# Reordering the unit pipeline of two attentions: transpositions and copies in front of the scores, outputs in the bank of the second transposed tile

## The chip, the cores and the metric

One NeuronCore of a Trainium2 chip runs the whole program. The metric is the device time of one execution in microseconds. The engines named here are TensorE (PE for its matmuls and PEld for its weight loads in the profile), VectorE (DVE), ScalarE (ACT), GpSimd (POOL) and SyncE (SP).

## The reference, cut to what matters

The program is one block of recurrent branches with a feed-forward part, and then two attention layers, all over 1024 tokens of width 1024 in 32-bit floats. The change touches two attentions of these layers: attention B (8 query heads on 2 key heads of width 64) and attention C (8 heads of width 96, values of width 64). Both are plain softmax attention over blocks of 128 queries:

```python
def one(qi):
    s = jnp.einsum('bqhgd,bkhd->bhgqk', qi, k).astype(jnp.float32) * scale
    p = jax.nn.softmax(s, axis=-1).astype(v.dtype)
    return jnp.einsum('bhgqk,bkhd->bqhd', p, v)
```

Attention D, in the second layer after C, subtracts one softmax from another. It isn't touched; the change gives B and C its order of work.

## The kernel before, in words

Attentions B and C each have 32 units. A unit b is a pair of heads (m = 0 and 1) at one block of 128 queries; 8 units in a row belong to one pair of heads p. For a unit there is this work:

- **S(b,0), S(b,1)**: TensorE makes the scores, 128 x 1024 each, in two banks of PSUM (line 1095 in B, line 1104 in C).
- VectorE takes the largest score of a row (line 2905) and makes a bias of it (helper, line 2167). ScalarE writes exp(scores) to SBUF (line 2061), which frees the bank of that S. VectorE takes the reciprocal of the sum (line 2925) and scales the probabilities (helper, line 2163, counted in `s_probs`).
- **T(b,0), T(b,1)**: TensorE transposes the probabilities, 8 tiles of 128 x 128 for each head (line 1126). ScalarE copies both to the tiles A(20) and A(21) (line 2071), which frees their banks.
- **O(b)**: TensorE multiplies values with A(20) and A(21), 32 small matmuls in one bank (line 1115). VectorE multiplies the result with the gate (helper, line 2159), which frees the bank.

There are four banks (`PS[0]` to `PS[3]`), given out in turn: the n-th job that TensorE opens (`opn`) takes bank n % 4 and must wait until the job n-4 was freed. `filled[i]` and `freed[i]` count per bank. Every engine takes its instructions strictly in the order of its own text, so the order of jobs sets both who shares a bank and who is queued behind whom.

Step s of the loop in `attend_pairs` does, before the change, on TensorE: S(s,0), S(s,1), O(s-2), T(s-1,0), T(s-1,1), so five jobs; on ScalarE: exp(s,0), exp(s,1), copy T(s-1,0), copy T(s-1,1); on VectorE: the maxima of S(s), the multiplication of O(s-2), the reciprocals and scalings of s. There are 34 steps.

`weave(main, side)` puts one piece of other work behind each step, on each engine. In B these are the projections of the next pair of heads (`prep_b`: behind steps 0, 8 and 16 a product `qb`; behind steps 1, 9 and 17 a rotation, a sum of squares `hq` and the product `gb` for the gate, all of `three`, line 336, but for the small ones) and behind steps 26 to 33 one eighth each of an output projection (`heads_out`, line 353, whose result VectorE adds to H in `half_in`, line 2159). Steps 2 to 7, 10 to 15 and 18 to 25 have nothing beside them on TensorE: 20 plain steps. In C every step up to 30 has side work: six times four pieces of `prep_c` (a product `qc`; `hq` with, for h = 4 and 6, the gate's product `gc`, and then a product `kc`; a sum `hn`; a spreading `hb`, with the product `vc` for even h), then seven pieces of `prep_d` (`qd`; `hq` and `kd`; `hn`; `hb`; `vd`; its transposition; `gd`). On ScalarE, a piece with a gate loads a table before the Silu and another one after it (lines 1832 and 1335), `kc` is followed by a copy, a square, and a copy and a square of the shared key (lines 1958 to 1965), `qc` by a copy, a square and two DMA issues, `qd` and `kd` by a copy, a square and four DMA issues (lines 1734, 1736, 1728, 1729). Ahead of the first unit of each pair of heads, `ready(p)` in C also waits until the keys of that pair were finished on VectorE, out of the bank of `hb`.

The order of TensorE around one step before:

```python
for s in range(nu + 2):
    if s < nu:            # S(s,0), S(s,1)
...
    if s >= 2:            # O(s-2), waits for both copies of T(s-2)
...
    if 1 <= s < nu + 1:   # T(s-1,0), T(s-1,1), each waits for s_probs
```

Of the kernel before, what the change touches and what calls it, by code (L numbers as in the profile page):

```python
# [11 lines left out]
ACT = mybir.ActivationFunctionType  # L12
AX = mybir.AxisListType

P = 128
# [3 lines left out]
NT = L // P  # L19
# [41 lines left out]
def build(nc, a):  # L61
    with ExitStack() as ctx:
# [26 lines left out]
        PS = [ctx.enter_context(nc.psum_tensor(f"ps{i}", [P, L], F32)) for i in range(4)]  # L89
        def sem(name):  # L90
            return ctx.enter_context(nc.semaphore(name))
# [79 lines left out]
        s_low_in = sem("low_in")  # L171
        s_kraw = sem("kraw")
        s_od_done = sem("od_done")
        s_turned = sem("turned")
        s_turned_out = sem("turned_out")
        s_lamv = sem("lamv")
# [4 lines left out]
        def A(i):  # L181
            return AR[:, i, :]
# [25 lines left out]
        J = {}  # L208
# [6 lines left out]
        def bank(name):  # L215
            return J[name] % 4

        def turn(name):
            return J[name] // 4 + 1
# [54 lines left out]
        def _(pe):  # L274
            def opn(name):
                n = njobs[0]
                njobs[0] += 1
                assert name not in J, name
                J[name] = n
                return PS[n % 4], n  # L280
# [790 lines left out]
            def att_a():  # L1071
# [2 lines left out]
                    pe.wait_ge(s_vs_in, 32 * (p + 1))  # L1074
                return attend_windows(ready)

            def attend_pairs(kind, q, k, v, ready):

                base = BASE[kind] = cnt["unit"]
                first = cnt["prob"]  # L1080
                nu = 32
                for s in range(nu + 2):
                    if s < nu:
                        b, p, u = base + s, s // 8, s % 8
                        if u == 0:
                            ready(p)
                        rows = slice(u * P, u * P + P)
                        if kind == "B":
                            two = [opn(("S", b, m)) for m in range(2)]
                            for pt, n in two:  # L1090
                                pe.wait_ge(freed[n % 4], n // 4)
                            for h in range(2):
                                for m, (pt, n) in enumerate(two):
                                    e = slice(m * 64, m * 64 + 64)
                                    mm = pe.matmul(pt[:, h * 512:h * 512 + 512], q(p, m)[e, rows],  # L1095
                                                   k(p, m)[e, h * 512:h * 512 + 512], start=True, stop=True)
                                    if h:
                                        mm.then_inc(filled[n % 4], 1)
                        else:
                            for m in range(2):  # L1100
                                pt, n = opn(("S", b, m))
                                pe.wait_ge(freed[n % 4], n // 4)
                                for h in range(2):
                                    mm = pe.matmul(pt[:, h * 512:h * 512 + 512], q(p, m)[0:96, rows],  # L1104
                                                   k(p, m)[0:96, h * 512:h * 512 + 512], start=True, stop=True)
                                mm.then_inc(filled[n % 4], 1)
                    if s >= 2:
                        b, p = base + s - 2, (s - 2) // 8
                        for m in range(2):
                            pe.wait_ge(freed[bank(("T", b, m))], turn(("T", b, m)))  # L1110
                        pt, n = opn(("O", b))
                        pe.wait_ge(freed[n % 4], n // 4)
                        for c in range(NT):
                            for m in range(2):
                                mm = pe.matmul(pt[m * 64:m * 64 + 64, 0:P], v(p, c, m), A(20 + m)[:, c * P:c * P + P],  # L1115
                                               start=c == 0, stop=c == NT - 1)
                        mm.then_inc(filled[n % 4], 1)
                    if 1 <= s < nu + 1:
                        b = base + s - 1
                        for m in range(2):  # L1120
                            pe.wait_ge(s_probs, first + 2 * (s - 1) + m + 1)
                            pt, n = opn(("T", b, m))
                            pe.wait_ge(freed[n % 4], n // 4)
                            pr = PROB[kind][(2 * (s - 1) + m) % 4]
                            for c in range(NT):
                                mm = pe.transpose(pt[:, c * P:c * P + P], pr[:, c * P:c * P + P], IDENT)  # L1126
                            mm.then_inc(filled[n % 4], 1)
                    yield
                cnt["unit"] += nu
                cnt["prob"] += 2 * nu  # L1130
# [192 lines left out]
        def _(act):  # L1323
            done = {}

            def tick(sem):
                done[sem.name] = done.get(sem.name, 0) + 1
                return done[sem.name]
# [720 lines left out]
            def attend_pairs(kind, scale):  # L2049
                base = cnt["unit"]  # L2050
                nu = 32
                for s in range(nu + 2):
                    if s < nu:
                        b = base + s
                        for m in range(2):
                            i = (2 * s + m) % 4
                            if s >= 2:
                                act.wait_ge(filled[bank(("T", b - 2, m))], turn(("T", b - 2, m)))
                            cnt["s"] += 1
                            act.wait_ge(s_negmax, cnt["s"])  # L2060
                            act.activation(PROB[kind][i], PS[bank(("S", b, m))][:, :], ACT.Exp, scale=row_scale(kind, s, m),  # L2061
                                           bias=SM[:, 20 + i:21 + i], accum_out=SM[:, 24 + i:25 + i])\
                                .then_inc(freed[bank(("S", b, m))], 1)
                            act.wait_ge(freed[bank(("S", b, m))], turn(("S", b, m)))
                    if 1 <= s < nu + 1:
                        b = base + s - 1
                        if s >= 2:
                            act.wait_ge(filled[bank(("O", b - 1))], turn(("O", b - 1)))
                        for m in range(2):
                            act.wait_ge(filled[bank(("T", b, m))], turn(("T", b, m)))  # L2070
                            act.activation(A(20 + m), PS[bank(("T", b, m))][:, :], ACT.Copy)\
                                .then_inc(freed[bank(("T", b, m))], 1)
                            act.wait_ge(freed[bank(("T", b, m))], turn(("T", b, m)))
                    yield
                cnt["unit"] += nu

# [1105 lines left out]
```

## Time and profile before

| what | value |
|---|---|
| device time, median of 3 runs | 3973.64 us (3968.29, 3973.64, 3984.16) |
| the profiled execution's own time | 3979.41 us |
| its span | 3977.6 us |
| TensorE busy | 3764.0 us, 95% of the span |
| VectorE busy | 1844.3 us, 46% |
| ScalarE busy | 1296.7 us, 33% |
| GpSimd busy | 914.3 us, 23% |
| granted TensorE clock, mean | 0.973 of full speed |
| attention B, first scores to last output | 2593.7 to some 2921 us of the span |
| attention C, first scores to last output | 3082.6 to 3476.9 us of the span |

A row of the timeline is: start, duration, engine, line, operation, output<-input, shapes and count, and in square brackets the idle time of the engine before it with what ended it. Matmuls are pipelined, so a group's duration runs a little into the next group's start; the distance from start to start is what a group costs TensorE. In a waits row, the instruction on the left waited for the one on the right: total, number of times, longest.

### The profile page before, as it was taken

How to read it: one execution, taken by the hardware profiler on the slowest of the kernel's cores; microseconds unless marked ns; L12 is line 12 of the kernel's file. 1: busy time of each engine (PE TensorE's matmuls, PEld its weight loads, DVE VectorE, ACT ScalarE, POOL GpSimd, SP SyncE). 2: the span in 40 equal slices, each digit the busy share in tenths (PEclk: the TensorE clock that was granted, in tenths of full speed). 3: DMA queues.
4: the chain of work that ended last, by engine and by line, in shares of the span. 5: the costliest groups of instructions: out<-in, count | busy, mean ns of one | idle time of the engine just before them, and what ended most of it. 6: DMA issues, size and time to landing. Idle time of an engine off the chain costs nothing.

```text
span 3977.6 us, 51609 instructions
## 1 busy us (share of the span) xinstructions
PE 3764.0 (95%) x21680; PEld 2965.5 (75%) x21680; DVE 1844.3 (46%) x2312; ACT 1296.7 (33%) x1520; POOL 914.3 (23%) x558
## 2 busy tenths in 40 slices
PE   7999999999999999999999899999999999988888
PEld 6778888877788778888888677767676566666667
DVE  7464555524733621101103556655744655465472
ACT  3244333332330011000001244455624665433341
POOL 4212222222233424333333311110022001111001
PEclk8999999999999999999999999999999999998899
DMA  4111111111125421111113211100121001010011
GB/s 138 37 43 51 46 53 44 49 53 46 48 87 191 124 85 48 48 48 48 48 50 110 82 42 48 37 18 10 51 84 32 14 12 40 19 25 19 16 54 66
DMA packets 276811, 215.30 MB, mean 54 GB/s; under 512 B 16272, under 2 KB 255024, under 8 KB 276592
## 3 DMA queue, kind: packets, MB, share of 16 engines
q1 hardware_dynamic: 256656, 146.11, 13.0%
q10 hardware_dynamic: 19936, 66.07, 4.6%
q8 instruction: 162, 2.65, 0.3%
q14 instruction: 57, 0.47, 0.0%
HBM read 170.27 MB, written 37.81 MB: 52 GB/s over the span
## 4 chain that ended last, share of the span: by engine, by line
PE 82%; DVE 10%; ACT 4%; issue 2%; ACTq 1%; DMA 0%; DVEq 0%; SPq 0%
PE ps L336 33%; PE ps L353 17%; PE ps L384 12%; DVE AR L2159 3%; PE ps L1104 2%; DVE SM L2905 2%; PE ps L603 2%; PE ps L318 2%; DVE AR L2167 2%; PE ps L1184 1%; PE ps L1115 1%; PE ps L1095 1%; PE ps L429 1%; PE ps L1126 1%; PE ps L295 1%
## 5 line engine op out<-in xcount | busy, mean ns | idle before, releaser
L3029 POOL CAST WH<-WR 128x1024 fp32r<-128x1024 f32 (+2 forms) x269 | 280.1, 1041 | 2925.8 <-DMA WR<-in_w_in 832.3
L3031 POOL TENSOR_TENSOR WL<-WR,WH 128x1024 fp32r<-128x1024 f32 (+2 forms) x269 | 595.6, 2214 | 21.6
L336 PE MATMUL ps<-XH,WH 128*128 128x512 f32 (+1 forms) x1968 | 499.2, 396 | 2.3 <-DVE AR L2159 1.7
L336 PE MATMUL ps<-XH,WL 128*128 128x512 f32 (+1 forms) x1968 | 488.8, 391 | 0.0
L336 PE MATMUL ps<-XL,WH 128*128 128x512 f32 (+1 forms) x1968 | 486.3, 389 | 0.0
L336 PEld LDWEIGHTS ps<-XH,WH 128*128 128x128 f32 (+1 forms) x1968 | 366.0, 188 | 86.6 <-issue 5.7
L336 PEld LDWEIGHTS ps<-XH,WL 128*128 128x128 f32 (+1 forms) x1968 | 369.3, 188 | 80.5
L336 PEld LDWEIGHTS ps<-XL,WH 128*128 128x128 f32 (+1 forms) x1968 | 367.1, 187 | 79.2
L2159 DVE TENSOR_TENSOR AR<-AR 128x512 f32<-128x512 f32 (+3 forms) x336 | 379.2, 1128 | 53.4 <-ACT AR L1593 38.0
L353 PE MATMUL ps<-ARR,WH 128*128 128x512 f32 x1600 | 396.1, 390 | 8.2 <-ACT ARR L1690 4.8
L353 PEld LDWEIGHTS ps<-ARR,WH 128*128 128x128 f32 x1600 | 300.5, 188 | 72.5 <-ACT ARR L1690 5.5
L2159 DVE TENSOR_TENSOR AR<-AR,ps 128x1024 f32<-128x1024 f32 (+2 forms) x72 | 84.7, 1176 | 544.8 <-PE ps L336 409.3
L2905 DVE TENSOR_REDUCE SM<-ps 128x1 f32<-128x1024 f32 x128 | 156.8, 1225 | 196.8 <-PE ps L1104 116.0
L2167 DVE SCALAR_TENSOR_TENSOR AR<-ps,AR 128x512 f32<-128x512 f32 (+2 forms) x122 | 59.3, 486 | 347.8 <-ACT AR L1348 239.7
L1708 ACT ACTIVATE AR<-ps 128x1024 f32<-128x1024 f32 x22 | 22.6, 1027 | 558.4 <-PE ps L336 558.4
L353 PE MATMUL ps<-ARR,WL 128*128 128x512 f32 x736 | 189.4, 392 | 0.0
L384 PE MATMUL ps<-XH,WH 128*128 128x512 f32 x672 | 185.7, 421 | 1.6 <-ACT AR L2002 1.6
L2061 ACT ACTIVATE AR<-ps,SM,AR 128x1024 f32<-128x1024 f32 x112 | 135.1, 1206 | 154.0 <-DVE SM L2167 147.8
L2163 DVE TENSOR_SCALAR AR<-AR,SM 128x1024 f32<-128x1024 f32 (+2 forms) x209 | 174.0, 833 | 7.3
L384 PE MATMUL ps<-XH,WL 128*128 128x512 f32 x672 | 167.3, 391 | 0.0
L384 PE MATMUL ps<-XL,WH 128*128 128x512 f32 x672 | 166.0, 389 | 0.0
L353 PEld LDWEIGHTS ps<-ARR,WL 128*128 128x128 f32 x736 | 139.3, 189 | 29.0
(254 smaller groups left out, 5135.9 us busy)
## 6 DMA issues: line engine op xcount, KB each, us to landing
WR<-in_w_in SPq DMA_DIRECT2D x78, 512.0 KB, 3.8
WR<-in_w_ffn_in SPq DMA_DIRECT2D x44, 512.0 KB, 3.8
spill<-H ACTq DMA_DIRECT2D x32, 512.0 KB, 2.7
gates<-AR ACTq DMA_DIRECT2D x32, 512.0 KB, 2.8
AR<-gates SPq DMA_DIRECT2D x32, 512.0 KB, 4.0
H<-spill ACTq DMA_DIRECT2D x32, 512.0 KB, 5.5
WR<-in_w_in_e SPq DMA_DIRECT2D x26, 512.0 KB, 3.9
WR<-in_w_in_o SPq DMA_DIRECT2D x23, 512.0 KB, 3.8
```

Of the source, the lines that this page charges most:

```text
L318: pe.matmul(pt[:, h * 512:h * 512 + 512], wp[:, slot, k, :], XH[:, k, h * 512:h * 512 + 512], start=k == 0 and wp is WH, stop=False, skip_ ...
L336: mm = pe.matmul(pt[0:m, h * 512:h * 512 + 512], wp[:, slot, k, 0:m], xp[:, k, h * 512:h * 512 + 512], start=i == 0, stop=i == 3 * KD - 1)
L353: mm = pe.matmul(pt[:, h * 512:h * 512 + 512], wp[:, w % 4, k, :], xp(k)[:, h * 512:h * 512 + 512], start=i == 0, stop=i == 3 * nk - 1)
L384: mm = pe.matmul(pt[:, h * 512:h * 512 + 512], wp[:, w % 4, k, :], xp[:, k, h * 512:h * 512 + 512], start=i == 0, stop=i == 3 * KD - 1)
L603: mm = pe.matmul(out, x1[r, c], later, start=True, stop=True)
L2061: act.activation(PROB[kind][i], PS[bank(("S", b, m))][:, :], ACT.Exp, scale=row_scale(kind, s, m), bias=SM[:, 20 + i:21 + i], accum_out=SM ...
L2159: return v.tensor_tensor(o, x, y, op)
L2163: return v.tensor_scalar(o, x, s1, None, op0)
L2167: return v.scalar_tensor_tensor(out=o, in0=x, scalar=s, in1=y, op0=op0, op1=op1)
L2905: v.tensor_reduce(SM[:, 34 + m:35 + m], PS[bank(("S", b, m))][:, :], AX.X, ALU.max)\
L3029: pool.tensor_copy(hi, full).then_inc(s_whi, 1)
L3031: pool.tensor_tensor(lo, full, hi, ALU.subtract).then_inc(s_wsplit, 1)
```

## The change

On TensorE, step s of `attend_pairs` now does T(s-2,0), T(s-2,1), S(s,0), S(s,1), O(s-2): the transpositions of the unit two back come first, and O(s-2) is written in the bank that T(s-2,1) had, after ScalarE copied it. So a step opens four jobs, not five. On ScalarE the two copies of T(s-2) come ahead of the exps of step s. VectorE's text is the same. Two new semaphores, `s_pair_turned` and `s_pair_out`, tell of T(b,1) and its copy, since that bank's own counters now belong to O(b). The transpositions are no longer made in step s-1; steps 32 and 33 have T and O of the last two units.

```diff
@@ TensorE, attend_pairs
+                    if s >= 2:
+                        b = base + s - 2
+                        for m in range(2):
+                            pe.wait_ge(s_probs, first + 2 * (s - 2) + m + 1)
+                            pt, n = opn(("T", b, m))
+                            pe.wait_ge(freed[n % 4], n // 4)
+                            pr = PROB[kind][(2 * (s - 2) + m) % 4]
+                            for c in range(NT):
+                                mm = pe.transpose(pt[:, c * P:c * P + P], pr[:, c * P:c * P + P], IDENT)
+                            mm.then_inc(s_pair_turned if m else filled[n % 4], 1)
+                        J[("O", b)] = J[("T", b, 1)]
                     if s < nu:
...
                     if s >= 2:
                         b, p = base + s - 2, (s - 2) // 8
-                        for m in range(2):
-                            pe.wait_ge(freed[bank(("T", b, m))], turn(("T", b, m)))
-                        pt, n = opn(("O", b))
-                        pe.wait_ge(freed[n % 4], n // 4)
+                        pe.wait_ge(freed[bank(("T", b, 0))], turn(("T", b, 0)))
+                        pairs_out[0] += 1
+                        pe.wait_ge(s_pair_out, pairs_out[0])
+                        pt = PS[bank(("O", b))]
...
-                        mm.then_inc(filled[n % 4], 1)
-                    if 1 <= s < nu + 1:
-                        b = base + s - 1
-                        for m in range(2):
-                            pe.wait_ge(s_probs, first + 2 * (s - 1) + m + 1)
-                            pt, n = opn(("T", b, m))
-                            pe.wait_ge(freed[n % 4], n // 4)
...
-                            mm.then_inc(filled[n % 4], 1)
+                        mm.then_inc(filled[bank(("O", b))], 1)
@@ ScalarE, attend_pairs
+                    if s >= 2:
+                        b = base + s - 2
+                        if s >= 3:
+                            act.wait_ge(filled[bank(("O", b - 1))], turn(("O", b - 1)))
+                        act.wait_ge(filled[bank(("T", b, 0))], turn(("T", b, 0)))
+                        act.activation(A(20), PS[bank(("T", b, 0))][:, :], ACT.Copy)\
+                            .then_inc(freed[bank(("T", b, 0))], 1)
+                        act.wait_ge(freed[bank(("T", b, 0))], turn(("T", b, 0)))
+                        act.wait_ge(s_pair_turned, done.get("pair_out", 0) + 1)
+                        act.activation(A(21), PS[bank(("T", b, 1))][:, :], ACT.Copy).then_inc(s_pair_out, 1)
+                        act.wait_ge(s_pair_out, tick(s_pair_out))
                     if s < nu:
...
-                            if s >= 2:
-                                act.wait_ge(filled[bank(("T", b - 2, m))], turn(("T", b - 2, m)))
...
-                    if 1 <= s < nu + 1:
-                        b = base + s - 1
-                        if s >= 2:
-                            act.wait_ge(filled[bank(("O", b - 1))], turn(("O", b - 1)))
-                        for m in range(2):
-                            act.wait_ge(filled[bank(("T", b, m))], turn(("T", b, m)))
-                            act.activation(A(20 + m), PS[bank(("T", b, m))][:, :], ACT.Copy)\
-                                .then_inc(freed[bank(("T", b, m))], 1)
```

## Rows read from the trace of the kernel before

**Rows 1.** Busy time by stretch (attention B, attention C): each engine, clock, DMA.

```profile
2593.70:2908.00 314.30, 294.82 (x2197) 214.36 (x2198) 199.26 (x325) 175.75 (x221) 27.22 (x24) 1.00 0.08 26
3082.50:3478.00 395.50, 376.69 (x2554) 255.11 (x2556) 217.41 (x368) 218.13 (x277) 34.02 (x20) 0.99 0.09 21
```

**Rows 2.** Waits of TensorE in the stretch of attention B.

```profile
PE ps L1095 <- ACT AR L2061: 5.9, 20, 0.5
PE ps L1126 <- ACT AR L2061: 4.9, 15, 0.4
```

**Rows 3.** Waits of TensorE in the stretch of attention C.

```profile
PE ps L1104 <- issue: 6.2, 4, 1.5
```

**Rows 4.** Timeline of one plain step of attention B.

```profile
2646.13 2.08 ACT L2071 ACTIVATE AR<-ps 128x1024 f32<-128x1024 f32 x2
2646.15 1.99 PE L1095 MATMUL ps<-AR 64*128 64x512 f32 x8 [0.30 <-ACT AR L2061]
...
2648.24 1.22 DVE L2905 TENSOR_REDUCE SM<-ps 128x1 f32<-128x1024 f32 x1 [1.09 <-PE ps L1095]
...
2648.31 1.97 PE L1115 MATMUL ps<-AR 128*64 128x128 f32 x32 [0.17 <-issue]
...
2650.21 2.07 PE L1126 MATMUL ps<-CST,AR 128*128 128x128 f32 x16
...
2651.15 0.29 DVE L2159 TENSOR_TENSOR AR<-ps,AR 128x128 f32<-128x128 f32 x1
2651.23 1.21 ACT L2061 ACTIVATE AR<-ps,SM,AR 128x1024 f32<-128x1024 f32 x1 [0.16 <-DVE SM L2167]
...
2652.58 1.99 PE L1095 MATMUL ps<-AR 64*128 64x512 f32 x8 [0.30 <-ACT AR L2061]
```

**Rows 5.** Timeline of a step of attention B with an output product behind it.

```profile
2852.81 1.07 PE L1126 MATMUL ps<-CST,AR 128*128 128x128 f32 x8 [0.45 <-ACT AR L2061]
...
2854.18 1.21 PE L353 MATMUL ps<-XH,WH 128*128 128x512 f32 x4 [0.30 <-ACT AR L2061]
...
2859.89 1.99 PE L1095 MATMUL ps<-AR 64*128 64x512 f32 x8
2860.06 1.22 DVE L2159 TENSOR_TENSOR H<-H,ps 128x1024 f32<-128x1024 f32 x1 [3.56 <-PE ps L353]
```

**Rows 6.** Timeline of attention B, TensorE alone: scores of units 8 and 11.

```profile
2665.63 1.99 PE L1095 MATMUL ps<-AR 64*128 64x512 f32 x8 [0.50 <-ACT AR L2061]
...
2710.88 1.99 PE L1095 MATMUL ps<-AR 64*128 64x512 f32 x8 [0.17 <-ACT AR L2061]
```

**Rows 7.** Timeline of attention C behind a gate's product and a key's product.

```profile
3194.96 1.28 ACT L1832 ACT_TABLE_LOAD   x1 [10.45 <-PE ps L336]
...
3196.64 3.70 PE L1104 MATMUL ps<-AR 96*128 96x512 f32 x8
...
3197.30 1.28 ACT L1335 ACT_TABLE_LOAD   x1
...
3201.87 1.05 ACT L1965 ACTIVATE AR<-AR 32x1024 f32<-32x1024 f32 x1
...
3205.72 1.09 PE L411 MATMUL ps<-AR,CST 96*64 96x128 f32 x16 [0.26 <-ACT AR L2061]
```

**Rows 8.** Timeline of attention C, TensorE alone: a key's step, a new pair.

```profile
3239.48 3.70 PE L1104 MATMUL ps<-AR 96*128 96x512 f32 x8
3243.11 1.97 PE L1115 MATMUL ps<-AR 128*64 128x128 f32 x32
...
3247.46 1.09 PE L411 MATMUL ps<-AR,CST 96*64 96x128 f32 x16 [0.39 <-ACT AR L2061]
...
3258.61 3.67 PE L1104 MATMUL ps<-AR 96*128 96x512 f32 x8 [1.54 <-issue]
```

**Rows 9.** Timeline of attention C, ScalarE alone: a DMA issue behind `kd`.

```profile
3399.17 0.63 ACTq L1728 DMA_DIRECT2D AR<-AR  x1
```

**Rows 10.** Busy time by stretch, as in rows 1: during the scores of unit 3 of C.

```profile
3109.70:3113.50 3.80, 3.80 (x7) 1.71 (x6) 0.88 (x3) 0.78 (x3) 0.00 (x0) 0.50 0.01 4
```

More of the change, by code:

```diff
@@ L173, in build @@
         s_od_done = sem("od_done")
+        s_pair_turned = sem("pair_turned")
+        s_pair_out = sem("pair_out")
         s_turned = sem("turned")
@@ L1075, in att_a @@
                 return attend_windows(ready)
+            pairs_out = [0]
             def attend_pairs(kind, q, k, v, ready):
@@ L1116, in attend_pairs @@
                                                start=c == 0, stop=c == NT - 1)
-                        mm.then_inc(filled[n % 4], 1)
-                    if 1 <= s < nu + 1:
-                        b = base + s - 1
-                        for m in range(2):
-                            pe.wait_ge(s_probs, first + 2 * (s - 1) + m + 1)
-                            pt, n = opn(("T", b, m))
-                            pe.wait_ge(freed[n % 4], n // 4)
-                            pr = PROB[kind][(2 * (s - 1) + m) % 4]
-                            for c in range(NT):
-                                mm = pe.transpose(pt[:, c * P:c * P + P], pr[:, c * P:c * P + P], IDENT)
-                            mm.then_inc(filled[n % 4], 1)
+                        mm.then_inc(filled[bank(("O", b))], 1)
                     yield
@@ L2064, in attend_pairs @@
                             act.wait_ge(freed[bank(("S", b, m))], turn(("S", b, m)))
-                    if 1 <= s < nu + 1:
-                        b = base + s - 1
-                        if s >= 2:
-                            act.wait_ge(filled[bank(("O", b - 1))], turn(("O", b - 1)))
-                        for m in range(2):
-                            act.wait_ge(filled[bank(("T", b, m))], turn(("T", b, m)))
-                            act.activation(A(20 + m), PS[bank(("T", b, m))][:, :], ACT.Copy)\
-                                .then_inc(freed[bank(("T", b, m))], 1)
-                            act.wait_ge(freed[bank(("T", b, m))], turn(("T", b, m)))
                     yield
```

## The prediction

> **What bounds the kernel now.** I read the page first: TensorE is busy for 95% of the span, and the chain that ended last is for the most part its matmuls. So a change of order can only give back time in which TensorE stands still in the two stretches that it touches. The busy time by stretch sizes that: in attention B 314.30 us with 294.82 busy, 19.5 us idle; in attention C 395.50 with 376.69 busy, 18.8 us idle [rows 1]. Together 38.3 us, 1% of the span. That is the ceiling of any gain.
>
> Next the waits of TensorE by stretch, to see who ends the idle time. In B they end with the exp (line 2061): 20 waits of the scores and 15 of the transpositions, of 0.5 us at most [rows 2]. In C the largest group is four waits of the scores of 1.5 us each, put down to issue [rows 3]; by their place three of them are `ready(p)`, which waits until VectorE has scaled the keys out of the bank of `hb` [rows 8].
>
> Then the timeline of one plain step of B, which is as regular as a clock: scores start at 2646.15 and again at 2652.58, so 6.43 us [rows 4]. TensorE's own work, from start to start, is 2.16 (scores, 1.92 where they come without a wait) + 1.90 (outputs) + some 1.80 to 1.85 (16 transpositions), 5.9 us. The rest is the end of a loop that runs scores (filled at 2.0), maximum 0, maximum 1, exp 1 (5.08 to 6.29 after the start), and then the next scores, which need the bank of exp 1. That loop sets the plain step, not TensorE.
>
> **The change, part by part.** Nothing is computed more or less often; only waits move. I write times from the start of the scores of a step, or from the end E of the side work, and follow who waits for which bank by counting jobs: four per step now, plus the side ones.
>
> *Plain steps of B, 20 of them.* The loop scores, maxima, exp 1, scores is not touched, since S(s+1,1) takes the bank of S(s,1) and, with four jobs, S(s+1,0) that of S(s,0). What is new lies inside it: TensorE does O(s-2) from 2.16 to 4.06, T(s-1,0) to 4.96, and T(s-1,1) must wait until VectorE has multiplied O(s-2), whose bank it takes. VectorE comes to that behind the two maxima, at 5.00 to 5.29 [rows 4]. So T(s-1,1) runs from about 5.35 to 6.25, and the scores come at 6.43 as before. The copies start when exp 1 has ended, as now, and end at 2.06 of the next step, in time for O at 2.16. Cost 0: the idle time is only split in two. The cover is thin, 0.2 us; if it fails, every tenth costs 2 us over these steps.
>
> *Steps 26 to 31 of B, with an output product behind them.* Before, the second transposition waits 0.45 us for exp 0 and the product 0.30 for exp 1 [rows 5], and from 2847.46 to 2859.89 (the scores before and behind) a step takes 12.43 us. With the new order the product takes the bank of T(s-2,0), long free, and the transpositions behind it find everything ready; S' needs the bank of the product, which VectorE empties at 0.17 + 1.22 us behind its end [rows 5], under the 1.80 of the transpositions. The step becomes 1.92 + 1.90 + 5.71 (2854.18 to 2859.89) + 1.80 = 11.33. Gain 1.1 x 6 = 6.6 us. In the last two steps there are no scores between T and O any more, so O waits for both copies: transpositions end at 1.8, copy 1 at about 3.15 (each is half of 2.08 us). Loss 1.35 x 2 = 2.7 us.
>
> *Steps with `qb` and `gb` in B.* Units 8 to 11 take 2710.88 - 2665.63 = 45.25 us [rows 6]. In the new order the waits for exp in front of `qb` and the rotation go. For them: behind `qb`, S' needs its bank, free after ScalarE's copy and square, 0.75 us later than the transpositions end; behind `gb` the Silu with its table load (1.28 + 1.02) keeps the bank 0.8 us longer than they cover, and the second load (1.28 [rows 7]) and the two copies then stand ahead of O, another 1.4 us. Walked through to the same point: 45.7 us, 0.45 more. Three such pairs, the first a little cheaper: +1.1 us.
>
> B in sum: -6.6 + 2.7 + 1.1 = -2.8 us.
>
> *C, where the copies come behind ScalarE's side work.* Here the moved copies have a price. The scores take 3.63 us, outputs 1.90 [rows 8], transpositions 1.80: 7.33 of work a step, above the loop of 6.4, so bare steps don't wait. Behind side work TensorE now reaches O at E + 1.8 + 3.6 = E + 5.4, and the copies (2.1 us) start only when ScalarE has done its part of the side work:
> - `qc` (copy, square, two DMA issues, 3.5 us): copies done at 5.8, stall 0.4; five such steps: +2.0, before none.
> - `kc` without a gate (copy, square, copy, square, some 4.5 us): done at 6.6, stall 1.2, four times.
> - `kc` behind a gate's product: ScalarE is through at 3201.87 + 1.05 = 3202.92, 6.3 us behind the start of the scores [rows 7]; stall E + 8.4 against 5.4 = 3.0, twice.
>  So 4 x 1.2 + 2 x 3.0 = 10.8. Before, the same six places take, from the scores to the `hn` behind them, 7.98 (twice, as 3239.48 to 3247.46 [rows 8]), 9.08 (twice, 3196.64 to 3205.72 [rows 7]), 9.47 and 9.98; less 7.33 each, 9.6 us of waits. Net +1.2.
> - `qd`, `kd`: copy and square, 2.2 us, and four DMA issues of 0.63 and a little [rows 9], 4.9 us; copies done at 7.0, stall 1.6 twice. `hn` behind them: 0.15, since VectorE's rotations get 1.8 us more. Together 3.35 against 4.1 before (8.55, 7.96 and 9.57 less 7.33). Net -0.75.
> - `ready(p)`: 1.54 us before [rows 8]; now the transpositions come first, but the scaling of the keys stands behind the second scaling of the probabilities, and about 0.9 is left. Three times: -1.9.
> - Steps 31 to 33: O(30) and O(31) wait for their copies before (1.50 and 1.42) and after; with the gate `gd` ahead, +0.3.
>
> C in sum: 2.0 + 1.2 - 0.75 - 1.9 + 0.3 = +0.85 us.
>
> *The rest.* Weight loads hang on the end of the product four back (SP's queue), whose order is the same and whose distances change by about a microsecond. GpSimd's splits follow them. Attention D and what follows start from the same state.
>
> **Sum.** -2.8 + 0.85 = -2.0 us. The profiled execution took 3979.41 us (span 3977.6); it would take 3977.4. It lies 5.8 us over the median of its three runs, so against the median I forecast 3973.6 - 2.0, about **3972 us**.
>
> **A row and a rule on the clock.** During the scores of unit 3 of C the granted clock was 0.50, the lower of its two levels, for 3.80 us; TensorE had just stood still, or nearly, for 1.4 us and 0.4 us [rows 10]. The eight matmuls took 6.16 us where others take 3.70. It fell once more, behind a 1.54 us wait at 3355, and not behind the other waits of that size. I count as many falls after as before. The Trainium skill (TensorE: Matmul & The Clock Gate, section Part 1: The HAM clock gate) says that the clock is lowered after idle stretches and only sustained activity brings the full rate back; the trace agrees at that place. By that rule alone the longer stalls of 3.0 us would each cost more than the stall, which speaks against this change; that is a rival below.
>
> **Rivals.**
> 1. *The waits really go.* If the copies and multiplications came in time everywhere, B and C would have no idle time: 38.3 us less, 3935 us. For it: the products of steps 26 to 31 do lose their waits. Against it: the plain steps are bound by a loop that the change leaves alone, and the copies stand behind ScalarE's side work. It would count from half of the ceiling on. Chance 0.07.
> 2. *The stalls lower the clock (slower).* Mechanism: O waits for late copies, TensorE idles, and the scores and products that follow run at half rate. There are 13 new or kept stalls of 1.2 us and more (five in B, eight in C). A fall costs half of the 3.80 us of [rows 10], 1.9 us: 13 x 1.9 = 25 us, so 3997 us. It decides from about 11 falls on. Against it: of four waits of 1.5 us in C only one was followed by a fall. Chance 0.05.
> 3. *T(s-1,1) behind the multiplication lengthens each step (slower).* If the wait on VectorE pushed the scores back by 0.5 us in the 60 steps, 30 us, 4002 us. Against it: 0.2 us of room in B by [rows 4], over 1 us in C. Chance 0.03.
>
> My forecast, waits that change places with no difference to be measured, has 0.85.
>
> **Range.** Its lower end: 3972 less 4 (no fall of the clock), less 6 (the stalls for copies, some 18 us in sum, a third smaller), less 5 (the spread of the runs before, 3968 to 3984, around its median): 3957. Its upper end: 6 for stalls a third larger, 6 for three more falls, and 6 for the spread: 3990. The rivals lie outside, with 0.15 in all. A measurement of this kernel tells about 0.5% from no change, 20 us: faster by more, 0.07 (rival 1); slower by more, 0.08 (rivals 2 and 3); within, 0.85.
>
> **What would show it.** Right: plain steps of B at 6.43 us, with T(s-1,1) waiting about 0.4 us for line 2159; steps 26 to 31 at 11.3; outputs (line 1115) that wait for line 2071 in C, 3 us behind both gates; idle time of TensorE in the two stretches within 5 us of 38.3. Wrong: plain steps above 6.6 (rival 3), a clock well under 0.98 in either stretch (rival 2), or idle time under 20 us (rival 1).

## The result and the profile after

| | before | after |
|---|---|---|
| device time, median of 18 runs each | 3973.57 us (3953.04 to 3984.16) | 3979.6 us (3975.33 to 3996.27) |
| the profiled execution, its span | 3979.41, 3977.6 us | 3977.78, 3976.0 us |

The ratio is 1.0028, with a 95% interval of 1.0015 to 1.0040: the changed kernel is slower by about 11 us by that ratio (the two medians lie 6.0 us apart, the two means 10.3), where 2 us less were forecast. The median lies in the range of the forecast, but its sign is wrong. The bound of 0.5% that the prediction gave for what can be told from no change was too wide: 18 runs of each resolve half of it.

The two profiled executions are a trap, for by them the new order is 1.6 us faster. Attention B begins at 2593.72 us of the span before and at 2587.60 after. That is 6.1 us ahead of any changed instruction, and more than the effect. So I compare stretches, each from its own first matmul. They are shown as [rows 1] are (window, length, busy time of each engine, granted clock, DMA). The three rows are attention B up to the first scores of C, C up to the first scores of D, and the rest.

```profile
2587.60:3077.99 490.39, 453.67 (x3059) 341.40 (x3059) 269.97 (x401) 232.66 (x285) 71.88 (x54) 0.98 0.13 39
3077.99:3477.33 399.34, 372.37 (x2549) 255.80 (x2549) 212.39 (x367) 218.11 (x277) 33.93 (x20) 0.99 0.09 21
3477.33:3976.00 498.67, 431.89 (x2394) 333.50 (x2392) 272.30 (x407) 172.59 (x227) 59.70 (x48) 0.94 0.12 36
```

The same three stretches of the kernel before:

```profile
2593.72:3082.58 488.86, 458.05 (x3059) 338.41 (x3059) 272.77 (x401) 232.73 (x285) 73.44 (x54) 0.98 0.12 39
3082.58:3476.86 394.28, 375.55 (x2548) 254.41 (x2549) 217.12 (x367) 218.13 (x277) 34.02 (x20) 0.99 0.09 21
3476.86:3977.60 500.74, 434.47 (x2394) 336.13 (x2392) 271.16 (x407) 172.59 (x227) 59.42 (x48) 0.93 0.12 36
```

B is 1.5 us longer, C 5.1 us, and the rest, which has the same text in both, is 2.1 us shorter. The idle time of TensorE (length less busy) went from 30.8 to 36.7 us in B and from 18.7 to 27.0 in C, 14 us more in the two together; since the busy time fell by 7.6 us, the two stretches grew by 6.6 us only. The prediction asked for less than 5 us of difference; its sign for a lost clock, a granted clock well under 0.98 in either stretch, did not show in this profile (0.98 and 0.99).

The changed kernel has other line numbers. 1095 is the transposition, 1110 and 1119 are the scores of B and of C, 1130 is the output product O. On ScalarE, 2063 and 2067 are the copies of the two transposed tiles, 2075 is exp, and 1741, 1837 and 1965 are the square behind a projection, the gate's Silu and the shared key's square. On VectorE, 2164 and 2172 are helpers.

Who ends the idle time is in the waits of TensorE, first for B and then for C (line after, line waited for: total, times, longest). They answer to [rows 2, 3].

```profile
PE ps L1130 <- ACT AR L2067: 14.2, 11, 1.5
PE ps L1095 <- DVE AR L2164: 4.2, 12, 0.5
PE ps L1110 <- ACT AR L1837: 3.1, 4, 0.8
PE ps L1110 <- ACT AR L1741: 1.3, 2, 0.7
...
PE ps L1130 <- ACT AR L2067: 21.7, 16, 2.7
PE ps L1119 <- ACT AR L2063: 2.5, 3, 0.9
PE ps L1119 <- DVE AR L2172: 1.8, 1, 1.8
```

The waits for exp are gone, as forecast. In their place O waits for the second copy (line 2067). The rows of B end at 2908 of the span, and one more such wait, of 1.47 us, follows at 2915.04. In sum there are 28 of them with 37 us, and 12 of the 28 are in B, where the forecast had five.

The timeline of B (start, duration, engine, line, operation, what ended the idle time before it) has them. The first row is the second transposition of a plain step. Then come the scores and outputs behind a gate; then step 19 with ScalarE's work around it, and the scores of step 26; then the scores of steps 27, 28 and 31 and the output of step 32:

```profile
2639.98 1.06 PE L1095 MATMUL ps<-CST,AR 128*128 128x128 f32 x8 [0.30 <-DVE AR L2164]
...
2699.30 1.99 PE L1110 MATMUL ps<-AR 64*128 64x512 f32 x8 [0.82 <-ACT AR L1837]
2702.70 1.97 PE L1130 MATMUL ps<-AR 128*64 128x128 f32 x32 [1.41 <-ACT AR L2067]
2706.49 1.99 PE L1110 MATMUL ps<-AR 64*128 64x512 f32 x8
...
2784.23 0.82 ACTq L1381 DMA_DIRECT2D H<-spill  x2
2785.06 1.99 PE L1110 MATMUL ps<-AR 64*128 64x512 f32 x8
2785.09 1.06 ACT L2107 ACTIVATE XH<-AR 128x1024 fp32r<-128x1024 f32 x1 [0.89 <-ACT AR L2075]
2786.18 1.02 ACT L2063 ACTIVATE AR<-ps 128x1024 f32<-128x1024 f32 x1
2787.23 1.02 ACT L2067 ACTIVATE AR<-ps 128x1024 f32<-128x1024 f32 x1
2788.40 1.97 PE L1130 MATMUL ps<-AR 128*64 128x128 f32 x32 [1.35 <-ACT AR L2067]
...
2833.74 1.99 PE L1110 MATMUL ps<-AR 64*128 64x512 f32 x8
...
2846.26 1.99 PE L1110 MATMUL ps<-AR 64*128 64x512 f32 x8
2857.52 1.99 PE L1110 MATMUL ps<-AR 64*128 64x512 f32 x8
...
2891.39 1.99 PE L1110 MATMUL ps<-AR 64*128 64x512 f32 x8
2904.17 1.97 PE L1130 MATMUL ps<-AR 128*64 128x128 f32 x32 [1.47 <-ACT AR L2067]
```

The rows at 2784 to 2788 are the ones to learn from. ScalarE issues two DMAs and rounds a tile of 1024 columns (line 2107) that a later product needs, and then copies. That rounding stands behind the exps, and so ahead of the next step's copies, in seven of the steps 18 to 25 (step 24 has none), and the two DMA issues stand ahead of it in the first four. Before the change the copies stood ahead of it. O then waits 1.35 to 1.44 us in steps 19 to 22, 0.50 in 23, 1.21 in 24, not at all in 25, behind the step without a rounding, and 1.21 in 26. From the scores of step 19 (2785.06) to those of step 26 (2833.74) a step takes 6.95 us. The same scores before the change, 6.68 us a step:

```profile
2788.58 1.99 PE L1095 MATMUL ps<-AR 64*128 64x512 f32 x8 [0.32 <-ACT AR L2061]
...
2835.34 1.99 PE L1095 MATMUL ps<-AR 64*128 64x512 f32 x8 [0.30 <-ACT AR L2061]
```

From 2857.52 to 2891.39 three steps take 11.29 us each, as forecast.

In C: O behind `qc`, O behind `kc`, the scores of `ready(p)`; behind a gate and `kc` the second half of the scores and O, and the same O one pair of heads later; O behind `qd` and behind `kd`, and the scores behind `hn` of the second layer:

```profile
3129.16 1.97 PE L1130 MATMUL ps<-AR 128*64 128x128 f32 x32 [0.61 <-ACT AR L2067]
3141.55 1.97 PE L1130 MATMUL ps<-AR 128*64 128x128 f32 x32 [1.35 <-ACT AR L2067]
3155.45 3.67 PE L1119 MATMUL ps<-AR 96*128 96x512 f32 x8 [0.84 <-ACT AR L2063]
3191.25 1.98 PE L1119 MATMUL ps<-AR 96*128 96x512 f32 x4 [0.47 <-ACT AR L1965]
3195.62 2.84 PE L1130 MATMUL ps<-AR 128*64 128x128 f32 x32 [2.39 <-ACT AR L2067]
3294.14 1.97 PE L1130 MATMUL ps<-AR 128*64 128x128 f32 x32 [2.39 <-ACT AR L2067]
3375.37 1.97 PE L1130 MATMUL ps<-AR 128*64 128x128 f32 x32 [2.66 <-ACT AR L2067]
3397.49 3.30 PE L1130 MATMUL ps<-AR 128*64 128x128 f32 x32 [2.06 <-ACT AR L2067]
3407.44 3.10 PE L1119 MATMUL ps<-AR 96*128 96x512 f32 x4 [1.83 <-DVE AR L2172]
```

**The clock** shows in these rows too. The same 32 matmuls took 2.84 us behind one wait of 2.39 us and 1.97 behind another. The granted clock (last column but two) in five such places:

```profile
3195.62:3198.18 2.56, 2.56 (x32) 2.56 (x34) 0.00 (x0) 2.48 (x4) 0.00 (x0) 0.68 0.00 0
3294.14:3296.04 1.90, 1.90 (x35) 1.90 (x37) 0.00 (x0) 1.87 (x3) 0.00 (x0) 1.00 0.00 0
3375.37:3377.26 1.89, 1.89 (x32) 1.72 (x32) 0.00 (x0) 1.86 (x3) 0.00 (x0) 1.00 0.05 9
3397.49:3400.52 3.03, 3.03 (x33) 3.03 (x35) 0.24 (x1) 2.48 (x4) 0.22 (x1) 0.57 0.02 5
3407.44:3410.48 3.04, 3.04 (x5) 0.83 (x5) 1.95 (x4) 0.89 (x1) 0.00 (x0) 0.62 0.00 0
```

Three of these five waits of 1.8 to 2.7 us were followed by the low level, and two were not, among them the longest.

**Two terms of every run.** Each run has its span and mean granted clock. At the low of its two levels the granted clock is 0.50 [rows 10], so a run lost about span x (1 - clock) to it, and its device time less that is its time at full clock. This is an estimate, since time in which TensorE waits at the low clock costs nothing; a straight line through the 87 runs below gives 0.94 us of device time for each us so counted. Over 87 runs of the kernel before, which were made beside the experiments, the time at full clock scatters by 2.5 us (standard deviation), the raw time by 6.5. This separates waits from clock for every kernel below, with a standard error of 0.7 us for 12 runs. What is lost to the clock scatters as the raw time does, and its mean over 12 runs has an error of 1.9 us:

| kernel (runs) | mean us | at full clock, against before | lost to the clock |
|---|---|---|---|
| before (87) | 3969.9 | 3872.9 | 97.0 |
| after (18) | 3982.6 | +7.8 | 102.0 |
| e1, B alone (12) | 3972.8 | +3.0 | 97.0 |
| e2, C alone (12) | 3982.4 | +4.0 | 105.5 |
| e3, O in its own bank (12) | 3985.7 | +6.5 | 106.2 |
| e4, side piece ahead, B 26 to 33 (12) | 3968.1 | -2.3 | 97.5 |
| e5, the same, 26 to 30 (11) | 3965.8 | -4.4 | 97.3 |
| e6, C's copies on VectorE (12) | 3972.4 | +0.6 | 98.9 |
| e7, e5 and e6 (12) | 3970.7 | -3.4 | 101.2 |
| e8, rounding behind copies (10) | 3976.5 | +3.1 | 100.6 |
| e10, e5 and C's key pieces (12) | 3960.9 | -7.7 | 95.7 |

So of the 12.7 us between these means, 7.8 are longer waits and 5.0 are more time at the low clock. The 7.8 are firm. The 5.0 are uncertain by some 2 us: against the 18 runs of the kernel before that belong to its own comparison the changed kernel is 10.3 us slower in the mean, not 12.7.

### The profile page after: what moved, and what is told of

Its sections match the earlier page's. It is cut to its first block, busy times and chain, and to the rows that moved or that the text cites. A ratio compares the mean times of both kernels' runs of the same rounds, so it can differ in the third digit from the quotient of the medians.

```text
span 3976.0 us, 51608 instructions
## 1 busy us (share of the span) xinstructions
PE 3751.8 (94%) x21680; PEld 2965.8 (75%) x21680; DVE 1834.0 (46%) x2312; ACT 1296.5 (33%) x1520; POOL 915.0 (23%) x558
## 4 chain that ended last, share of the span: by engine, by line
PE 84%; DVE 7%; ACT 6%; issue 1%; ACTq 1%; DMA 0%; DVEq 0%; SPq 0%
PE ps L338 33%; PE ps L355 17%; PE ps L386 12%; PE ps L1130 2%; DVE AR L2164 2%; PE ps L605 2%; PE ps L320 2%; PE ps L1119 2%; PE ps L1095 1%; DVE AR L2172 1%; PE ps L1189 1%; PE ps L1110 1%; PE ps L297 1%; PE ps L431 1%; DVE SM L2910 1%
## 5 line engine op out<-in xcount | busy, mean ns | idle before, releaser
L1130 PEld LDWEIGHTS ps<-AR 128*64 128x64 f32 x2048 | 114.1, 139 | 87.5 <-issue 87.5
L2168 DVE TENSOR_SCALAR AR<-AR,SM 128x1024 f32<-128x1024 f32 (+2 forms) x209 | 162.1, 776 | 7.3
```

Of the source, the lines that this page charges most:

```text
L2168: return v.tensor_scalar(o, x, s1, None, op0)
```

## The experiments

Line numbers of T, O and the copies shift in some of these kernels; what each is, is said. "At full clock" for a stretch is its length less half of its time at the low clock.

### Which of the two attentions: e1 and e2

Each keeps the old text for one attention and the new one for the other:

```diff
-            def attend_pairs(kind, q, k, v, ready):     # one order for both
+            def attend_pairs_b(kind, q, k, v, ready):   # e1: new order; e2: old order
+            def attend_pairs_c(kind, q, k, v, ready):   # e1: old order; e2: new order
```

> Attention B in the new order, attention C in the old one. From the two traces, the stretch from the first scores of B to the last output product beside it is 327.3 us before and 329.3 us after; C is 394.3 and 399.3. Theory 1 (late copies on ScalarE are what costs, most of it in C): B alone gives +2 us, stretch of B 329.3, stretch of C 394 as before; 3975 to 3976 in time. Theory 2 (the second transposition, which waits on VectorE's multiplication because it gives its bank to the outputs, costs in each step): most of the 6 to 11 us lies in B, which has its waits in nearly all steps; stretch of B above 331. Theory 3 (the extra time is in neither stretch, but in the clock of attention D and of what follows): both single changes are the same as before in their stretches.

> Attention C in the new order, B in the old one. Theory 1: +5 us, stretch of C 399 us against 394.3, with outputs (line of the 32 small matmuls) waiting 1.35 us behind each kc, 2.4 us behind each gate, 2.1 to 2.7 us behind qd and kd; time 3978 to 3980. Theory 2: C gains or stays, since it has more than 1 us of room for the multiplication. Theory 3: stretch 394 to 395, and the time still above before.

Measured: B alone 3974.23 us, ratio 1.0010 (0.9994 to 1.0027); C alone 3982.98 us, ratio 1.0028 (1.0015 to 1.0041). C alone has the ratio of the whole change, and B alone can't be told from no change by its raw time. C alone costs clock, 8.5 us (with an error of 2), and B none. At full clock the two add 3.0 and 4.0 us, 7.0 of the 7.8. In the profile of e1, B has the same 329.3 us as in the changed kernel, as its first theory had it. The stretch of C in the profile of e1 (old order) and of e2 (new order):

```profile
3081.76:3471.41 389.65, 372.16 (x2549) 253.30 (x2549) 216.06 (x367) 217.96 (x277) 34.01 (x20) 1.00 0.09 22
```

```profile
3077.60:3483.27 405.67, 378.41 (x2548) 259.62 (x2549) 212.82 (x367) 217.94 (x277) 33.91 (x20) 0.97 0.09 21
```

16 us lie between them, of which 10 are the clock (0.97 against 1.00): at full clock C takes 393.9 with the new order and 388.0 with the old.

### Is it the shared bank: e3

O gets a bank of its own again, in the new order, so that a step opens five jobs:

```diff
-                            mm.then_inc(s_pair_turned if m else filled[n % 4], 1)
-                        J[("O", b)] = J[("T", b, 1)]
+                            mm.then_inc(filled[n % 4], 1)
...
-                        pt = PS[bank(("O", b))]
+                        pt, n = opn(("O", b))
+                        pe.wait_ge(freed[n % 4], n // 4)
```

> Both attentions in the new order, but the outputs in a bank of their own (five jobs a step again), so that the second transposition no longer waits for VectorE's multiplication of the outputs before. Theory 1: about the time of the changed kernel, 1 us less at most (plain steps of B 6.43 us in place of 6.47); the waits of the outputs for ScalarE's copies stay, 1.35 and 2.4 us in C. Theory 2: the extra time goes, 3973 us, ratio 1.000 to the kernel before.

Measured: 3986.35 us, ratio 1.0037 (1.0023 to 1.0051). At full clock 1.3 us under the changed kernel, hardly more than the error of 0.9 us. Behind the gate in C the same waits stand, 0.47 and 2.34 us:

```profile
3196.18 1.98 PE L1173 MATMUL ps<-AR 96*128 96x512 f32 x4 [0.47 <-ACT AR L2019]
3200.51 1.97 PE L1184 MATMUL ps<-AR 128*64 128x128 f32 x32 [2.34 <-ACT AR L2150]
```

So the outputs over the second transposed tile cost next to nothing, and it is the order that costs.

### Where the gain of steps 26 to 31 comes from: e4 and e5

The old order everywhere, but in B the side piece comes ahead of the transpositions, in steps 26 to 33 (e4) or 26 to 30 (e5):

```diff
+                    ahead = kind == "B" and 26 <= s < 31     # e4: s >= 26
+                    if ahead:
+                        yield
                     if 1 <= s < nu + 1:                      # T(s-1,0), T(s-1,1)
...
-                    yield
+                    if not ahead:
+                        yield
```

> The kernel before, with one thing of the new order: in steps 26 to 33 of B the output product is put ahead of the transpositions of the same step (scores, outputs, product, transpositions). My reading of the gain that the new order has in these steps is that the product and the transpositions behind it no longer wait for exps; then a step takes 11.3 us in place of 12.4, six times, and the last two steps don't stall on copies: 7 us less than before, 3966 to 3967 us, ratio 0.998. Rival: the gain comes from the four-job rotation of the banks, or the product now waits for the bank of a transposed tile; then steps stay above 12 us.

> The kernel before, with the output product ahead of the transpositions only in steps 26 to 30 of B. In the run with steps 26 to 33, the steps of 26 to 31 were 11.3 us as expected, but the outputs of steps 32 and 33 each waited 1.42 us, since the transpositions then stood right in front of them. My theory: with five steps and the last three as before, all of the gain of 1.2 us a step stays, 6 us in the stretch of B (321 us against 327.3), time 3965 to 3967. Rival: the gain of the earlier run was within the noise and this one is 1.000 too.

Measured: e4 3967.32 us, ratio 0.9996 (0.9981 to 1.0010); e5 3965.67 us, ratio 0.9989 (0.9978 to 0.9999). By these intervals e4 can't be told from no change and e5 barely can; their times at full clock, 2.3 and 4.4 us under the kernel before, and the profiles can. A step with an output product takes 11.3 us in both, as with the new order. In e4 both last outputs then wait for copies made too late, as in the changed kernel and against what was expected, so that the gain is a third of the 7 us (waiter L1119 is O there):

```profile
2916.04 1.97 PE L1119 MATMUL ps<-AR 128*64 128x128 f32 x32 [1.42 <-issue]
```

Leaving the last steps as they were (e5) gives 2.1 us of that back, by the times at full clock, and B from its first scores to the product behind its last output takes 321.6 us where 321 was expected. So the gain of the forecast, 6.6 less 2.7 us, needs none of the rest of the change; it comes from the product standing between the exps and the transpositions.

### Is it ScalarE's queue: e6, e7, e8 and e9

e6 has the old order in B and the new one in C, with C's copies made by VectorE; e7 adds e5:

```diff
-                        act.activation(A(20), PS[bank(("T", b, 0))][:, :], ACT.Copy)
+                        v.tensor_copy(A(20), PS[bank(("T", b, 0))][:, :])
```

> B as before; C in the new order, but VectorE copies the transposed tiles, ahead of its maxima, in place of ScalarE. Theory 1 (the outputs wait because the copies stand behind ScalarE's side work): the waits of the outputs behind qc (0.61 us, five), kc (1.35, four), the gates (2.4, two), qd and kd (2.1 to 2.7) go for the most part, and C, 394 us at full clock in the changed kernel and 388 to 389 before, comes down to some 380 us; time 3962 to 3966, ratio 0.998 or less. VectorE's rotations behind kc leave a wait of about 0.5 us. Rival (the order itself costs, by the bank shared with the outputs or by VectorE's multiplication): C stays at 394 us or above, and VectorE, with 2.3 us more a step, makes it longer still: 3983 and more.

> The two together: B in the old order with the product ahead in steps 26 to 30, C in the new order with VectorE's copies. If both hold, their gains add up: 6 + 8 = 14 us or more less than before, 3958 us, ratio 0.9965. If C with VectorE's copies is no gain, it is as long as the worse of the two plus or minus the 6 us of B.

Measured: e6 3970.99 us, ratio 1.0010 (0.9998 to 1.0023); e7 3970.75 us, ratio 1.0003 (0.9993 to 1.0013). The output behind the gate waits no more:

```profile
3191.05 1.98 PE L1174 MATMUL ps<-AR 96*128 96x512 f32 x4 [0.47 <-ACT AR L2020]
3192.97 1.97 PE L1185 MATMUL ps<-AR 128*64 128x128 f32 x32
```

Of the 4.0 us that the new order costs in C at full clock, 3.4 are gone (e2 against e6, with an error of 1). But more was expected, C at some 380 us: it takes 389.4 us at full clock, no less than with the old order, for the waits moved. In e6 nine outputs wait 9.4 us for VectorE's copies, 3.6 the longest (a tenth, with 1.70, follows behind the window of these rows), and the scores of `ready(p)` wait as long as in the old order:

```profile
PE ps L1185 <- DVE AR L2989: 9.4, 9, 3.6
PE ps L1174 <- issue: 6.0, 4, 1.5
```

No kernel with C in the new order beat the same kernel with C in the old one: e7 took 3970.75 us and not the 3958 that was hoped for, and is slower than e5.

e8 is the changed kernel with ScalarE's side piece (the rounding, line 2107) behind the exps moved behind the copies of the next step, in steps 18 to 25 of B:

```diff
                         act.wait_ge(s_pair_out, tick(s_pair_out))   # the two copies are made
+                    if kind == "B" and s >= 19:
+                        yield
...
-                    yield
+                    if kind != "B" or s < 18:
+                        yield
```

> The changed kernel, with one thing moved on ScalarE in B: from step 18 on its side work (the rounding copies of steps 18 to 25, 1.06 us each) runs between the two copies of the transposed tiles and the exps of the next step, where ScalarE is idle, in place of ahead of the copies. My forecast forgot these rounding copies. Theory: steps 18 to 25, 6.95 us on average in the changed kernel, come back to 6.47, 3.5 to 4 us less in B, and the outputs there wait no longer for ScalarE. Rival: the exps are now late, and the steps stay at 6.9 or more.

Measured: 3976.33 us, ratio 1.0020 (1.0003 to 1.0037); at full clock 4.7 us under the changed kernel. In the profile the stretch from B's first scores to C's is 4.2 us shorter at full clock (single profiles of one text differ there by up to 2.6 us). A step from 19 to 25 takes 6.64 us on average (6.95 in the changed kernel, 6.47 expected), and step 26 takes 11.43 in place of 12.52. O starts without a wait, and only the second transposition waits for VectorE. Three rows, T(s-1,1), S and O:

```profile
2786.30 1.06 PE L1095 MATMUL ps<-CST,AR 128*128 128x128 f32 x8 [0.52 <-DVE AR L2167]
2787.37 1.99 PE L1110 MATMUL ps<-AR 64*128 64x512 f32 x8
2789.48 1.97 PE L1130 MATMUL ps<-AR 128*64 128x128 f32 x32
```

e9 is the changed kernel with every gate a plain copy, so that ScalarE loads no tables around it. It leaves out the Silu of all gates:

```diff
-                act.activation(dst, PS[bank(name)][:, :], other(ACT.Silu)).then_inc(freed[bank(name)], 1)
+                act.activation(dst, PS[bank(name)][:, :], ACT.Copy).then_inc(freed[bank(name)], 1)
```

> The changed kernel, with every gate computed by a plain copy in place of the Silu, so that ScalarE loads no tables around a gate (it leaves out the Silu of all gates). If what the gates add in the new order is ScalarE's queue (function tables and gate ahead of the copies of the transposed tiles), then in C the output products behind the two gates wait for the copies 1.35 us (as behind a key's copy without a gate) in place of 2.39, and the 0.47 of the second scores goes: 1.5 us twice, C 3 us shorter at full clock, about 391. In B the waits of 0.82 and 1.41 us behind each of the three gates go: 6.6 us, and B about 484. Rival: the waits are not ScalarE's queue but VectorE's multiplies, and stay within 0.3 us of what they were.

Measured, one run: 3983.71 us, at a mean clock of 0.971. The waits of C came as expected, 1.35 us behind both gates and no wait of the scores; at full clock C takes 390.4 us (391 expected). In B the waits of 0.82 and 1.41 us are gone as well, but units 8 to 11 shorten by 1.52 us only (46.05 to 44.53), not 2.2, since 0.52 us of a wait for VectorE comes up behind them. B as a whole, up to the first scores of C, is 3.3 us shorter at full clock, half of the 6.6 expected. The total is higher than the changed kernel's, but the clock took some 115 us of this run, against 102 there; at full clock the run is 12 us under the changed kernel. It is one run, and other gates of the program lose their tables too. The output behind the first gate of C:

```profile
3201.69 1.97 PE L1130 MATMUL ps<-AR 128*64 128x128 f32 x32 [1.35 <-ACT AR L2067]
```

### What beats both: e10

e5 for B, and C in the old order with the side piece ahead of the transpositions in steps 7, 15 and 23, where `hb` of the next pair is made (the recorded text calls B's order new in steps 26 to 31; it is the old one with the product put ahead, as in e5):

```diff
-                    ahead = kind == "B" and 26 <= s < 31
+                    ahead = 26 <= s < 31 if kind == "B" else s in (7, 15, 23)
```

> Attention B as in the kernel with the new order in steps 26 to 31 alone plus the old order elsewhere, as in the fifth experiment, and in C, in the old order, the side piece ahead of steps 7, 15 and 23 is put in front of the transpositions. If the wait of 1.54 us in which the scores behind a scaled key wait is only VectorE's chain begun too late, it falls to about 0.6 us in the three places: C 2.8 us shorter at full clock (386 to 387), total some 8 us under the kernel before, ratio about 0.998. Rivals: the wait stays at 1.5 us because the key piece is set by the other scaling; or C is shorter at full clock and the gain is lost in more time at the low clock (ratio 0.999 to 1.000).

Measured: 3960.84 us, ratio 0.9979 (0.9965 to 0.9994), about 8 us under the kernel before. The scores of `ready(p)` wait 0.98, 0.98 and 0.85 us, where 0.6 was expected and [rows 8] have 1.54; of 2.8 us hoped for 1.8 came. Two rows, the transpositions, now behind the side piece, and the scores of the new pair:

```profile
3150.42 1.97 PE L1192 MATMUL ps<-CST,AR 128*128 128x128 f32 x16
3153.37 3.67 PE L1167 MATMUL ps<-AR 96*128 96x512 f32 x8 [0.98 <-issue]
```

At full clock C takes 386.8 us, 1.9 less than the mean of four profiles with the old order (388.7); the clock took no more than before.

## Why the prediction was wrong, point by point

**B, forecast -2.8 us, measured +2.0** from the first scores to the product behind the last output (327.3 to 329.3 us; e1 has the same 329.3).
- *Plain steps, "Cost 0".* This is the first step that failed: "The copies start when exp 1 has ended, as now". For the bare steps it holds: 6.46 us against 6.43, with the second transposition 0.30 us behind line 2164, where 0.4 was forecast. But of the 20, seven of the steps 18 to 25 are not bare on ScalarE. Their rounding of 1.06 us, in four of them with two DMA issues, now stands ahead of the copies, and the cover of 0.2 us that I called thin fails: O waits 1.35 to 1.44 us behind the four, and 0.50 to 1.21 behind the other three. A step takes 6.95 us against 6.68, +1.9 us in seven of them, and step 26, whose copies come behind the last rounding, keeps 12.52 us and gains nothing: 1.2 us of forecast gain missed. e8 takes the rounding out of the way, and 4.7 us at full clock come back. I had looked at what stood beside these steps on TensorE, and not at ScalarE's own side pieces.
- *Steps with an output product, 11.33 us.* Right: 11.23 to 11.38. The steps from 27 on gained 1.25 us each (four of them took 45.13 us in place of 50.12). e4 and e5 show that the mechanism was the one named.
- *The last two steps, 2.7 us.* 2.9 (1.47 twice).
- *`qb` and `gb`, 0.45 us a pair.* 0.80 (45.25 to 46.05): the waits are the ones forecast, 0.67 behind `qb` (0.75), 0.82 and 1.41 behind `gb` (0.8 and 1.4), but less of the old idle time went.

**C, forecast +0.85 us, measured +5.3 at full clock** (388.7 to 393.9, means of four profiles each). Of the 4.4 us between:
- *`qd`, `kd` and the `hn` behind, "stall 1.6 twice" and "0.15".* Mis-sized, the largest term: 2.66, 2.06 and 1.83, together 6.55 against 3.35, so 3.2 us. One DMA issue behind `qd` took 1.19 us where [rows 9] have 0.63, and one had taken 1.18 there before the change. Behind `kd` all four took 0.63, and still O came 7.4 us behind the start of the transpositions (3390.09 to 3397.49) where 7.0 were reckoned. VectorE finishes with `hn`'s bank only behind three rotations of 3.75 us in sum, while the scores that want it come early.
- *`qc`, 0.4.* 0.61, five times: 1.05 us.
- *`kc`, 1.2 and 3.0.* Right: 1.35 four times and 0.47 + 2.39 twice, 11.1 us against 10.8. e9 confirms the 1.5 us of the tables.
- *`ready(p)`, 0.9.* Right: 0.84 and 0.85 (twice).
- *Steps 31 to 33, +0.3.* 0.8: three outputs wait 0.76, 1.47 and 1.47 us, where two waited 1.50 and 1.42.

**The clock, "I count as many falls after as before".** This step failed as well, and it makes 5.0 of the 12.7 us. In one profile each of before and after the low clock in C does last equally long, 10.2 us. But over five profiles with the new order and ScalarE's copies in C (after, e2, e3, e8, e9) it lasted 10.2, 23.6, 17.1, 10.2 and 27.0 us, over five with the old order (before, e1, e4, e5, e10) 10.2, 3.4, 13.4, 10.2 and 3.4. The means differ by 9.5 us, worth half of it in time, 4.7; with values that scatter so, five on each side give the sign and not the size. The runs agree: the clock takes nothing more with B alone, 8.5 us more with C alone. Rival 2 had the mechanism, and no more than a fifth of its 25 us came. Its price of 1.9 us a fall was too low for the fall that it was read from: there the clock stayed at 0.50 for 6.8 us, of which [rows 10] show 3.80, so that fall was worth 3.4 us. The rule of the Trainium skill (TensorE: Matmul & The Clock Gate, section Part 1: The HAM clock gate) that idle stretches lower the clock agrees with this in its direction; two of the five waits above were followed by no fall. No run changed the length of these waits alone. That their length brings the falls is argued from e2 against e6, where the clock's share falls from 105.5 to 98.9 us with the waits (101.2 in e7), and not shown: each share has an error of 1.9 us, and in the profiles of e6 and e7 the low clock in C lasts 13.7 and 16.7 us, hardly less than the 17.6 of the five.

**In sum**: 4.8 us missed in B, 4.4 in C and 5.0 from the clock make 14.2 of the 14.7 us between the forecast of -2.0 and the +12.7 of the means. (By the comparison of 18 runs each, with +10.3 us, the clock's part would be 2 to 3 us.) The forecast took "waits that change places" for a balance without checking each queue that the copies moved behind: they moved ahead of the exps, but with that to the end of whatever ScalarE does behind the exps of the step before.

## What to carry to other kernels

- When an instruction is moved in an engine's text, list everything that this engine executes between its old and its new place in every kind of step, side pieces and DMA issues too. A step that is bare on the bounding engine can be full on another.
- Time at full clock (device time less span x (1 - clock)) scatters far less than the raw time and parts new waits from lost clock; single spans don't decide about 10 us in 4000.
- Before a whole order is changed for one gain, try the one move that makes it: five steps of B and three of C with the side piece put first gave 8 us, where the new order lost 11.

## What the hardware showed that was not expected

- The same waits were followed by the low clock at one time and not at another: 2.39 us with a fall at 3195 and without one at 3294, 2.66 us without and 1.83 us with one, in one execution. In the stretch from D's first scores to the end, whose text is the same in all kernels but for the gates of e9, the low clock took 50 to 77 us over twelve profiles.
- TensorE at the low clock slowed short and long matmuls alike: 32 outputs took 2.84 to 3.30 us in place of 1.97, and 4 scores 3.10 in place of 1.98.
- A DMA issue on ScalarE's queue is not one price: 0.63, 0.67 and 1.19 us within one piece (behind `qd`), and in e9 two issues that take 0.82 us in the changed kernel took 1.69, 0.87 more, ahead of an output product that waited 2.95 us where it had waited 1.35.
